# Expert matmuls in unsplit fp32 on two 64-column halves of TensorE, with weight chunks of 1 MB

## The reference, cut to what matters

```python
def _expert_choice_ffn(h, w_router, w_e_gate, w_e_up, w_e_down):
    cap = EC_CAPACITY * s // N_EXPERTS                 # 2 * 512 / 16 = 64 tokens for each expert
    aff = jax.nn.softmax(h @ w_router, axis=-1)
    vals, idx = lax.top_k(jnp.swapaxes(aff, 1, 2), cap)
    xg = jax.vmap(lambda hb, ib: hb[ib])(h, idx)       # 16 experts x 64 tokens x 2048
    a = jnp.einsum('becd,edf->becf', xg, w_e_gate)     # 2048 -> 1024
    u = jnp.einsum('becd,edf->becf', xg, w_e_up)       # 2048 -> 1024
    y = jnp.einsum('becf,efd->becd', jax.nn.silu(a) * u, w_e_down)   # 1024 -> 2048
    y = y * vals[..., None]
    return scatter_add(idx, y)                         # back to 512 tokens x 2048
```

## Time and profile before

| | |
|---|---|
| Time, median of 2 runs | 2672.13 us (2668.15 and 2676.11) |
| Span of the profiled execution, first to last instruction | 2677.6 us; the page gives no other time for it |
| TensorE busy over the span | 2451.8 us, 92% |
| VectorE, ScalarE | 1578.6 us, 59% and 1144.4 us, 43% |
| Moved by DMA | 629.78 MB, mean 235 GB/s |
| Mean granted clock of TensorE | 0.979 of 2.4 GHz |

### The profile page before, as it was taken

One profiled execution on the slowest core, in us unless ns is written; L12 is line 12 of the kernel. 1 busy time (PEld: TensorE's weight loads), 2 busy tenths in 40 slices (PEclk: granted clock), 3 DMA queues, 4 the chain that ended last, 5 costly groups with the idle time before them and its releaser, 6 DMA issues.

```text
span 2677.6 us, 32386 instructions
## 1 busy us (share of the span) xinstructions
PE 2451.8 (92%) x10344; PEld 1752.1 (65%) x10344; DVE 1578.6 (59%) x1763; ACT 1144.4 (43%) x1625; POOL 122.8 (5%) x85
## 2 busy tenths in 40 slices
PE   0699997999999999999996999999999999999996
PEld 0588876788744447888764766667575766767654
DVE  6732269766523364353346677676767667676767
ACT  2243421222233362122224665656465655656565
POOL 0000059100000010000000000000000000000000
PEclk9899999999999999999998999999999999999998
DMA  9833386878711003444213999999899999999996
GB/s 332 316 110 95 119 252 208 310 274 324 253 36 35 0 0 118 155 137 142 79 63 131 347 333 337 336 327 333 307 342 334 335 325 331 335 326 330 337 359 241
DMA packets 311252, 629.78 MB, mean 235 GB/s; under 512 B 30278, under 2 KB 38748, under 8 KB 309468
## 3 DMA queue, kind: packets, MB, share of 16 engines
q1 hardware_dynamic: 306044, 618.81, 66.0%
q10 hardware_dynamic: 4608, 8.39, 0.8%
q0 software_dynamic: 480, 1.05, 0.4%
HBM read 615.59 MB, written 12.58 MB: 235 GB/s over the span
## 4 chain that ended last, share of the span: by engine, by line
PE 77%; DVE 10%; DMA 5%; issue 4%; ACT 4%; SPq 0%; ACTq 0%; DVEq 0%
PE bank L530 16%; PE bank L765 14%; PE bank L532 13%; PE bank L774 8%; PE bank L771 7%; PE bank L742 4%; DMA ada_tile<-in_w_ada 3%; DVE w_lo L1533 3%; PE bank L616 2%; PE bank L785 2%; ACT w_hi L1101 2%; DVE ada_acc L1242 2%; DVE acc_first L1242 1%; PE bank L583 1%; PE bank L663 1%
## 5 line engine op out<-in xcount | busy, mean ns | idle before, releaser
L1533 DVE TENSOR_TENSOR w_lo<-stage,w_hi 128x1024 fp32r<-128x1024 f32 x510 | 616.0, 1223 | 233.2 <-ACT w_hi L1101 230.1
L1101 ACT ACTIVATE w_hi<-stage 128x1024 fp32r<-128x1024 f32 x510 | 530.1, 1053 | 297.1 <-PE bank L774 263.0
L1209 DVE TENSOR_TENSOR w_lo<-stage,w_hi 128x1024 fp32r<-128x1024 f32 (+1 forms) x170 | 223.6, 1316 | 370.8 <-ACT w_hi L868 370.1
L868 ACT ACTIVATE w_hi<-stage 128x1024 fp32r<-128x1024 f32 (+1 forms) x170 | 177.0, 1043 | 606.1 <-PE bank L530 377.9
L765 PE MATMUL bank<-stage,xgT 128*128 128x512 f32 x672 | 316.8, 594 | 0.0
L771 PE MATMUL bank<-w_hi,xgT 128*128 128x512 f32 x688 | 279.8, 488 | 9.0 <-ACT w_hi L1101 5.6
L774 PE MATMUL bank<-w_lo,xgT 128*128 128x512 f32 x688 | 220.6, 402 | 8.2 <-DVE w_lo L1533 6.5
L1242 DVE SCALAR_TENSOR_TENSOR ada_acc<-ada_tile,siluc,ada_acc 128x1024 f32<-128x1024 f32 x120 | 183.9, 1532 | 17.4 <-DMA ada_tile<-in_w_ada 14.5
L765 PEld LDWEIGHTS bank<-stage,xgT 128*128 128x128 f32 x672 | 125.9, 190 | 94.6 <-issue 82.2
L771 PEld LDWEIGHTS bank<-w_hi,xgT 128*128 128x128 f32 x688 | 123.3, 191 | 92.4 <-issue 62.1
L530 PE MATMUL bank<-hT_hi,w_lo 128*128 128x512 f32 x512 | 162.5, 399 | 18.2 <-DVE w_lo L1209 18.2
(11 more groups left out here) (242 smaller groups left out, 3479.4 us busy)
## 6 DMA issues: line engine op xcount, KB each, us to landing
stage<-in_w_e_gate SPq DMA_DIRECT2D x256, 512.0 KB, 5.8
stage<-in_w_e_up SPq DMA_DIRECT2D x256, 512.0 KB, 5.6
stage<-in_w_e_down SPq DMA_DIRECT2D x256, 512.0 KB, 6.5
ada_tile<-in_w_ada SPq DMA_DIRECT2D x192, 512.0 KB, 5.3
stage<-in_w_in SPq DMA_DIRECT2D x96, 512.0 KB, 5.4
stage<-in_w_out SPq DMA_DIRECT2D x32, 512.0 KB, 3.5
sig_gates<-sig ACTq DMA_DIRECT2D x32, 256.0 KB, 2.9
stage<-in_w_br_a SPq DMA_DIRECT2D x16, 512.0 KB, 5.7
```

Source lines behind the costliest of these rows:

```text
L868: A(w_hi[:, c % NSPLIT, :, 0:width], stage[:, c % NSTAGE, :, 0:width], ACT.Copy).then_inc(hi_ready, 1)
L1101: A(w_hi[:, s, :, :], stage[:, c, :, :], ACT.Copy).then_inc(hi_ready, 1)
L1209: V.tensor_tensor(w_lo[:, c % NSPLIT, :, 0:width], stage[:, c % NSTAGE, :, 0:width], w_hi[:, c % NSPLIT, :, 0:width].bitcast(F32), ALU.sub ...
L1533: V.tensor_tensor(w_lo[:, s, :, :], stage[:, cc % NSTAGE, :, :], w_hi[:, s, :, :].bitcast(F32), ALU.subtract)\
```

## The change

Every expert chunk is multiplied in plain float32, with no split of weights or tokens. A chunk is now one 128-row tile of **both** experts of the pair by 1024 columns: 1 MB, in rows of 4 KB. There are 48 in a pair. The stationary operand is the 64 tokens of one expert (64 columns). Expert 0 writes PSUM partitions 0 to 63 and expert 1 partitions 64 to 127 of the same two banks, that is, they use the two column halves of TensorE. A chunk has four matmuls: expert 0 for both 512-column halves of the weights, then expert 1 for both. The ring is 12 slots of 1 MB (96 KB of each partition), taken from the old ring, from the place of the removed buffers and from the `ada` region; `x1` moves by 5 KB. The `fold` goes; silu(gate) x up is computed in the token layout (`sg`) and transposed by TensorE (8 transposes in a pair). `gather` for the next pair is placed in and after the up and down chunks, `scatter` at two places of this pair and two of the next. The gate row's diagonals are made by GpSimd and its four matmuls run in the routing stage.

```diff
+EC, NSLOT = 48, 12
+USES = EC // NSLOT
-    w_gate_v = w_e_gate[0].rearrange("e (k p) n -> e p k n", p=P)
+    w_gate_v = w_e_gate[0].rearrange("e (k p) n -> k p e n", p=P)
...
+        xgT = at("A", 0, "xgT", [P, KD, 2, CAP])
+        heT = at("A", 8 * KB, "heT", [P, 8, P])
+        e_slot = [at("ring", 8 * i * KB, f"e_slot{i}", [P, 2, 2 * W]) for i in range(6)]
...
+            def load_expert_chunk(p, c):
+                if c < 32:
+                    src = (w_gate_v, w_up_v)[c // KD][c % KD][:, ds(2 * p, 2), :]
+                else:
+                    half, kc = (c - 32) // 8, c % 8
+                    src = w_down_v[kc][:, ds(2 * p, 2), half * 2 * W:(half + 1) * 2 * W]
+                sp.dma_start(e_slot[c % NSLOT][:, :, :], src).then_inc(e_full[c % NSLOT], 16)
...
+                for cc in range(EC):
+                    sp.wait_ge(e_used, EC * p + cc - NSLOT + 1)
+                    load_expert_chunk(p, cc)
...
+            def expert_chunk(p, c, b0, tokens, first, end):
+                slot = c % NSLOT
+                pe.wait_ge(e_full[slot], 16 * USES * p + 16 * (c // NSLOT) + 16)
+                for e in range(2):
+                    for h in range(2):
+                        last = mm(bank[b0 + h][64 * e:64 * e + 64, :], tokens[e], e_slot[slot][:, e, h * W:(h + 1) * W],
+                                  start=first, stop=end)
+                last.then_inc(e_used, 1)
...
+                pe.wait_ge(selT_ready, p + 1)
+                pe.wait_ge(val_ready, p + 1)
+                if not last_pair:
+                    pe.wait_ge(sel_ready, p + 2)
+                    gather(4, 0)
+                for j in range(2):
+                    pe.wait_ge(he_ready, 2 * p + j + 1)
                     for f in range(4):
+                        last = nc.tensor.transpose(bank[6 + j][:, f * P:(f + 1) * P], sg[:, j, f * P:(f + 1) * P], ident[:, :])
+                    last.then_inc(tr_done, 1)
+                if not last_pair:
+                    gather(5, 1)
+                pe.wait_ge(silu_ready, 2 * p + 2)
+                for half in range(2):
+                    for kc in range(8):
+                        if half == 0 and kc % 4 == 0:
+                            pe.wait_ge(heT_ready, 2 * p + kc // 4 + 1)
+                        expert_chunk(p, 32 + 8 * half + kc, 2 * half, [heT[:, kc, 64 * e:64 * e + 64] for e in range(2)],
+                                     kc == 0, kc == 7)
...
+                        if half == 1 and kc == 3:
...
+                            scatter(p, 0)
+                scatter(p, 1)
...
-            def hi_expert(p, e, cc):
...
-                A(w_hi[:, s, :, :], stage[:, c, :, :], ACT.Copy).then_inc(hi_ready, 1)
...
-            def lo_expert(p, e, cc):
...
-                V.tensor_tensor(w_lo[:, s, :, :], stage[:, cc % NSTAGE, :, :], w_hi[:, s, :, :].bitcast(F32), ALU.subtract)\
-                    .then_inc(lo_ready, 1)
...
+            def second_half(p):
+                y_scaled(p, 2)
+                y_rest(p, 2)
+                add_scattered(p, 1)
+                y_scaled(p, 3)
+                y_rest(p, 3)
+                add_scattered(p, 2)
+                add_scattered(p, 3)
```

More of the change, by code:

```diff
@@ L461, in load_pair @@
[L461 to L474, removed]
@@ L731, in _ @@
             last.then_inc(affT_done, 1)
+            pe.wait_ge(acc_free, G_EXP + 4)
+            for q in range(4):
+                pe.wait_ge(diag_ready, 5 + q)
+                mm(bank[q][:, :], ones[:, :], diag1[q][:, :, :], start=True, stop=True).then_inc(row_done, 1)
             pe.wait_ge(slotT_ready, 1)
@@ L735, in _, with gather @@
             last.then_inc(slots_done, 1)
-            def gather(b, u, tiles=range(4)):
-                for i in tiles:
+            def gather(b, u):
+                for i in range(4):
                     for t in range(T):
@@ L754, in scatter @@
+                    mm(bank[4 + t][:, :], selT[:, t * P:(t + 1) * P], y_lo[jd % 2][:, :], start=False, stop=True)\
                         .then_inc(scat_done, 1)
[L756 to L769, removed]
-                    for kk in range(2):
-                        mm(bank[b][:, :], acts[kk], w_hi[:, s, kk, :], start=first and kk == 0, stop=False)
-                    pe.wait_ge(lo_ready, k + 1 + NSTAGE)
-                    for kk in range(2):
-                        last = mm(bank[b][:, :], acts[kk], w_lo[:, s, kk, :], start=False, stop=end and kk == 1)
-                last.then_inc(chunk_used, 1)
@@ L777, in fold @@
-            def fold(p, e, jb):
-                pe.wait_ge(acc_free, G_EXP + 16 * p + 8 * e + 2 * jb + 6)
-                if jb == 0 and e == 0 and not (isinstance(p, int) and p == 0):
-                    pe.wait_ge(scat_added, 16 * (p - 1) + 4 * sum(c < FOLD_AT[0] for c in SCATTER_AT) + 4)
-                for s in range(2):
-                    for f in range(4):
-                        last = mm(bank[4][:, s * 256 + f * 64:s * 256 + (f + 1) * 64], gu[:, s, f * P:(f + 1) * P],
-                                  foldm[:, :], start=True, stop=True)
-                last.then_inc(fold_done, 1)
@@ L852, in _ @@
                 gather(4 + u, u)
[L853 to L857 removed]
+            pe_pair(0, True, False)
+            with pe.Fori(1, PAIRS - 1) as p:
+                pe_pair(p, False, False)
+            pe_pair(PAIRS - 1, False, True)
+            for jd in (2, 3):
+                scatter(PAIRS - 1, jd)
         @block.scalar
@@ L1079, in _, with tokens @@
                 normalised(t)
-            def tokens(turn, b, u, count):
-                act.wait_ge(gather_done, count)
-                if not isinstance(count, int) or count > 1:
-                    act.wait_ge(xg_ready, count - 1)
+            act.wait_ge(x1_ready, 16)
+            for q in range(4):
+                act.wait_ge(row_done, 5 + q)
+                A(gt_row[:, q * W:(q + 1) * W], bank[q][:, :], ACT.Copy).then_inc(row_ready, 1)
+            def tokens(p, u, b):
+                act.wait_ge(gather_done, 4 * p + u + 1)
@@ L1564, in add_scattered @@
-            def add_scattered(p, jd, tiles=range(T)):
-                for t in tiles:
+                V.tensor_tensor(y_lo[jd % 2][:, :], y32[jd % 2][:, :], y_hi[jd % 2][:, :].bitcast(F32), ALU.subtract)\
+                    .then_inc(ylo_ready, 1)
+            def add_scattered(p, jd):
+                for t in range(T):
                     dve.wait_ge(scat_done, 16 * p + 4 * jd + t + 1)
```

422 lines of the change are left out of this document (147 added, 275 removed).

## The result

The changed kernel takes **2431.07 us** (median of 2 runs, 2428.87 and 2433.26) against 2672.13 for the kernel before (2 runs, 2668.15 and 2676.11). The ratio is 0.9092, 95% interval 0.9065 to 0.912: 9% faster, where 1% was forecast.

A forecast was written before the change was run, and what follows sets the result against it. TensorE was taken to bound the expert stage. 2677.6 - 16 (eight pairs) - 15 (first pair) + 2 (tail) = 2648.6, cross-checked at 2652; forecast 2645 us, -1.0%, 8-in-10 range 2435 to 2760, own case 2615 to 2720.

The forecast's parts named there:

- The bound before: Expert stage before the change: TensorE bounds it at 152.0 us a pair, with transfers 7% behind.
- Chunks on TensorE: Expert matmuls: halves overlap only at switches, 2.58 us a chunk, 123.8 us a pair for 48 chunks.
- my own rival: Expert stage: halves overlap fully at 1.72 us a chunk, transfers bound at 126 us a pair, 2440 us; chance 0.37.
- Other work, 25.2 us a pair: TensorE beside the chunks: folds go; gather, scatter, selection and affinities stay; eight transposes (1.8 us) come; 25.2 us a pair.
- Gaps: TensorE's waits in a pair: w_hi and w_lo waits vanish, new ones mostly covered; 1 us a pair taken.
- Transfers: Expert weight loads in 4 KB rows: 400 GB/s, 126 us a pair, hidden under TensorE's 149.
- First pair: Routing and start of the first pair: chunk wait, `lo` steps and gate row matmuls save about 15 us.
- The two `lo` steps: Router's chain before the first pair: two steps of 1.2 us each go, saving 2.4 us.
- the gate row: Four gate row matmuls, 3.4 us, move under the router's VectorE steps, where TensorE is idle.
- Tail: From the last chunk to the kernel's end: 30 us against 29 before, counted as +2 us.
- my case: Expert stage: overlap at the switches alone, TensorE still the bound, 150 us a pair, 2645 us; chance 0.42.
- The second rival: Expert chunks: little or no overlap of the halves, 3.44 us a chunk, 190 us a pair, 2975 us; chance 0.21.

The follow-up runs named there:

- b_narrow: Kernel before the change, with weight loads cut to 64 of 512 columns from the second pair on; 2670.9 us.
- n_run1: Changed kernel, loads cut to 64 of 1024 columns from the second pair on, scatters and selection transposes after chunks 7, 11 and 15; 2323.23 us, ratio 0.8696.
- n_onehalf: As n_run1, but expert 1 also writes expert 0's partitions, so both experts use the same column half; 2983.35 us.
- alt: Changed kernel with all its loads, the four matmuls of a chunk alternating between the experts; 2424.84 us, ratio 0.9076.
- slots4: Changed kernel with four ring slots of 1 MB instead of twelve, rows still 4 KB; 2531.13 us, ratio 0.9468.
- rows2k: Changed kernel with each chunk loaded by two 512 KB transfers in rows of 2 KB; 2485.18 us, ratio 0.9287.

## Why the prediction was wrong, by its own steps

- **The bound before: right.** b_narrow shows it: 151.6 us a pair without transfers.
- **Chunks on TensorE: this step failed.** It took the order that the earlier trace rows show on the whole array as a rule across halves: "a matmul whose half is taken holding back all behind it", six places for eight records, 2.58 us. The runs show that order holds back only behind a fourth waiting record. Six places is what d = 0 gives for runs of 4; with d = 3 four in a row is the longest run that costs nothing, and the chunk is 1.77 us. The error is 48 x (2.58 - 1.73) = 41 us a pair on TensorE. The transfers let 28.6 of it through (150 forecast, 121.4 found), in seven pairs 200 of the 214 us by which the forecast (2645) missed. The row that spoke for it was in my own rival: a record 0.02 us behind an unsplit one can be read as a waiting place. I had named it and then asked for two such places before I would believe it.
- **The rule.** The starts at 1724.397 and 1724.410 us are the first and the fifth record in program order, by the reading above, ahead of the second. The Trainium skill, TensorE: Matmul & The Clock Gate, section "What overlaps and what doesn't", has matmuls start and end in program order, strict FIFO. Across halves the trace does not agree, and the measurement decides; within a half no run here contradicts it.
- **Other work, 25.2 us a pair: right.** n_run1 has 109.3 against 48 x 1.72 + 25.2 = 107.8. The chunks in its chain add up to 84.0 us a pair (27.67 + six of 7.07 + 13.94), which leaves 25.3 for the rest.
- **Gaps: right in kind.** In 880 us the only new wait for something else than a chunk is one of 0.9 us for `sg`; none for `heT` or `y_lo`. n_run1, where TensorE has no time to spare, shows none at all from 1600 to 2200 us. The waits of TensorE in 1500 to 2380 us (total, times, longest):

```profile
PE bank L741 <- DMA e_slot<-in_w_e_up: 67.1, 109, 0.7
...
PE bank L785 <- DVE sg L1468: 0.9, 1, 0.9
```

- **Transfers: 400 GB/s taken, 406 to 409 found,** and no longer hidden. The Trainium skill, DMA: Bandwidth & Descriptors, section "iDMA fabric — 4 AXI ports for 8 engines, asymmetric across TPBs", in its table of a load stream beside iDMA reads, has 408.7 GB/s for such a stream alone, of 1 MiB DMAs in rows of 4 KiB; the windows agree (407 and 409).
- **First pair: -15 forecast, 15.6 found, the shares wrong.** The gap to the first `selT` shrank by 22.7 us. Of this 7.1 is there at 1061 us, in the merge of the mixer, up to where the change touches only the place of `x1` and two later loads of `x`, which I had put at nothing. The tile `m_tmp` of the kernel before, and of the changed one:

```profile
L1409 DVE TENSOR_TENSOR m_tmp<-bank,sg_in x16: 684/692/692, 1061.3 to 1200.1; 128x512 f32<-128x512 f32 x16
```

```profile
L1314 DVE TENSOR_TENSOR m_tmp<-bank,sg_in x16: 682/691/692, 1054.2 to 1193.1; 128x512 f32<-128x512 f32 x16
```

These 7.1 us are not the change's. b_narrow, which has the code of the kernel before up to there, has the first start at 1054.9, and kernels with the changed code have it from 1045.0 (n_run1) to 1057.2 (n_onehalf), alt, slots4 and rows2k at 1048.3, 1053.1 and 1055.3. Two executions of the same code differ by 6.4 and more, so the 7.1 is scatter between executions, "nothing" was right, and 22.7 - 7.1 = 15.6 is left for the first pair. The two `lo` steps brought 0.8 us (the first MAX8 is 7.9 us earlier, 7.1 of it as above), not 2.4. The gather and the first four chunks after:

```profile
1420.16 10.35 PE bank L721 x64
1430.51 7.07 PE bank L741 x32
```

The gather became longer (10.35 against 8.88). TensorE had been idle but for 0.6 us from 1409.3 to 1420, and the granted clock was 0.50 (1.2 GHz) there and for the gather's first 6 us, at 0.213 us a matmul; after that it was 1.00, at 0.112. In the kernel before 3 us of the gather ran at 0.50; in alt, whose code is the same up to there, the gather took 8.75. So the first chunk starts 6.4 us earlier, less than the 7.1 of scatter. From the first chunk to the first `selT` it is 31.1 us against 47.4, 16.3 less. The wait of 8.9 us for a chunk did go. The other 7.4 are more than the 3.4 of the gate row; 13 chunks at 1.77 us in place of split and unsplit ones are in it too, and I have not told the two apart.
- **Tail: 30 us forecast, 30.3 found,** from the last chunk's end at 2400.88 to 2431.2, but partly by luck. Up to the square root I had added up the steps for `y` and VectorE's additions, with 0.7 for the squares, 14.9 us from the last chunk on. The chain has 14.3, but from 2403.67 to 2415.14 it is ScalarE's squares (L1060, 0.73 us a piece), with one piece each of `y_hi`, `y_lo` and an addition in between.

```profile
2398.90 1.98 PE bank L741 x8
...
2415.16 1.28 ACT L1099
```

- **The rivals.** The first is right in mechanism, pair (124.0, or 121.4 in the mean, against 126) and time (2431 against 2440). It had 0.37, my case 0.42; its sign was a record already begun while another ran, and that of mine was an order seen on the whole array alone, so 0.42 was too much. The range went wrong at its lower end by the same choice: it began 5 us below the rival's figure at 400 GB/s, though 405 stood in the earlier trace rows: 390 MB at 405 are 963 us, 12 less than at 400, and the rival's time 2428. The second rival's price was right (3.45 us a chunk, 191.3 a pair against 190) and its case did not occur. A slip without consequence: 2.47 to 2.75 us a chunk around a forecast of 2645 is 2603 to 2710 us, not 2615 to 2720.

No version beats the change by more than a measurement can tell: with 1.03 of DMA share at 408 GB/s from 1458 to 2371 us, an order that saves TensorE time saves nothing.

## What to carry to other kernels

A rule of order that the trace shows for the whole array need not hold between tiles of the array: before pricing by it, look for a record that begins while another runs, and keep half the chance for the case that the rule lets through. When a change takes work from the engine that bounds, work out what the next resource gives at its best row in the trace, and set the end of the range beyond it. Look at the pace of each repetition and not at the mean alone: here the first pair ran at TensorE's pace and the later ones at the transfers'. Where two column halves are used, keep at most four matmul records (two float32 matmuls) of one half in a row, which costs nothing. In these kernels 8 cost a lag at the start of each stretch, 16 two thirds of what the overlap gives TensorE ((164.7 - 109.3) / (191.3 - 109.3)), and 32 all of it (204.6, other waits included).

## What was not expected of the hardware

- Three waiting records, by count: 16 of 512 columns or 32 of 256 in a row both let the other half start when three are left (12.22 us for 32, 13.15 us for 64).
- A float32 matmul with 64 stationary columns streams at the pace of one with 128 (0.43 us a record of 512), and two at once, on both halves, take nothing from each other: 0.216 us a record over 128 records.
- Rows of 2 KB move at 386 GB/s with up to 24 transfers of 512 KB queued, against 354 in the stage before with at most eight; rows of 4 KB at 406 to 409 with twelve slots of 1 MB. With four slots they reach 410 while TensorE frees slots, and 378 and 372 over whole windows of 300 us.
